# The state update's matmuls directly behind the turn in every unit of the Mamba-2 stage

## The chip, the cores and the metric

One Trainium2 chip, one of its cores. TensorE multiplies, VectorE, ScalarE and GpSimd do the elementwise work, SyncE issues most transfers. The metric is the time of the whole program on the device in microseconds (us), as the median of several executions; lower is better.

## The reference

Three blocks, each a residual layer over 1024 tokens of width 1024, run one behind the other. The change lies in the third block's Mamba-2 (SSD) mixer, and in the stage that computes it. Cut to that, the reference is:

```
h = rms_norm(x, norm_g);  proj = h @ w_in
xbc = silu(causal_depthwise_conv(xbc_raw, conv_w, conv_b))        # 4 taps
xs, bm, cm = split(xbc);  dt = softplus(dt_raw + dt_bias)
x_dt = xs * dt;  a_cs = cumsum(dt * a_head) within each chunk of 128 tokens
y_diag = sum over s <= l in the chunk of (C_l . B_s) exp(a_cs[l] - a_cs[s]) x_dt[s]
states[c] = sum over l in chunk c of B_l exp(a_cs[last] - a_cs[l]) x_dt[l]
state entering chunk c+1 = exp(a_cs[last of c]) * state entering c + states[c]
y_off = C_l . (state entering the chunk) * exp(a_cs[l])
y = (y_diag + y_off + xs * d_skip) * silu(z)
merged = g_sb * (y_sb @ w_out_sb) + g_ssd * (rms_norm(y) @ w_out_ssd) + g_rw * (y_rw @ w_out_rw)
x = x + merged @ w_o
```

There are 16 heads of 64 columns, two groups of 8 heads that share B and C (64 states each), and 8 chunks of 128 tokens. The gated output projections of the two other branches (`y_rw @ w_out_rw`, `y_sb @ w_out_sb`) need nothing of the Mamba-2 branch.

## The kernel before

Features lie on the 128 partitions and the 1024 tokens along them (`T` = 1024, `P` = `C` = 128, `NCH` = 8 chunks). Each stage is a set of per-engine programs written out by hand, in which each engine runs its own list in order, and waits on semaphores where it needs another engine's result. Nothing plans the order: it is the order of the calls.

The stage is `ssd_branch`. It runs 8 units `u`, each one pair of heads (128 feature rows). PSUM is held as four areas of 128 x 1024: `A` for the output, `F` for the projection that is computed alongside, `X` for the transposed input and `U` for the state sums. TensorE's list of a unit has five parts:

- `turn(u)` (L2814): 8 transposes that bring `xs` of the unit, once ScalarE has put the silu on it, into `X`.
- `fill(u, begin, end)` (L595, in `multiply_two`): matmuls `begin` to `end - 1` of the 48 that project one weight tile of the other two branches. Each is 128x128 by 512 tokens, and there are three for each product, because float32 is split in a high and a low part (`y_hi`, `y_lo`, and the stream's `w_hi`, `w_lo`). They fall in four sums of 12: part 0 first half of tokens, part 0 second half, part 1 first half, part 1 second half. `F` has room for two of them, so the third sum (from matmul 24) waits until ScalarE has copied the first out (`keep(u, 0)`), and the fourth (from matmul 36) until `keep(u, 1)` has copied the second. This is the wait on the semaphore `kept`.
- `update(u)` (L2826): 14 matmul instructions in the trace (7 chunks), the sums over each chunk of B times the decayed input, into `U`. It first waits for `x_ready(u)`, which VectorE gives at the end of `take_x(u)`.
- `products(u)` (L2838, L2840): the rest of the unit, 60 matmul instructions that need the state, the masked attention and a free `A`.
- `turn(u + 1)` ends the unit.

The order in the unit is written in the loop at L2843:

```
turn(0)
for u in range(units):
    first = 0 if u == 0 else 16
    fill(u, 0, first)
    update(u)
    fill(u, first, 48)
    products(u)
    if u + 1 < units:
        turn(u + 1)
```

So unit 0 has the update directly behind the turn already, and units 1 to 7 have 16 of the 48 projection matmuls between them.

VectorE's list of a unit: wait for the products of the unit before; `take_x` (L2939 scales the turned input by dt into `xdt`, L2942 by the decay into `xend`, two instructions each, then `x_ready`); `take_out` of the unit before (L2947); `advance_state` (L2953, L2955, L2958, which ends in `state_ready`); `gate(u, 0)` and `gate(u, 1)` (L2970, which multiply what `keep` copied by a gate); `finish` (L2975); `convolve(u + 1)` (L2920, L2922); `gate(u, 2)` and `gate(u, 3)`; `mask(u + 1)` (L2931). Behind `mask(4)` comes `cut_last(1)` (L2979), the last of four splits of the second branch's input into high and low part.

ScalarE's list of a unit: `clamp(u + 1, 0)` (L2866, 8 instructions); `keep(u, 0)` (L2885); `clamp(u + 1, 1)`, `decays(u + 1)` (L2874: a table load and two exponentials of 128x1024); `keep(u, 1)`; a table load and the silu of z (L2903); `keep(u, 2)`; `keep(u, 3)`; `round_y(1)` in unit 3 only (L2879); `silu(u + 1)` (L2858). Unit 7 has no clamp and no decays.

GpSimd splits the streamed weight tiles (`cut_tile`, L546 and L548), and in units 0 and 4 three of the four input rows (L2805). At unit 4 TensorE's first projection matmul also waits for that split (`y_cut`, in `fill`, wherever it is called with `begin` 0 and `end` above 0). SyncE's queue loads convolution inputs, z, decay rows, gates and one weight tile a unit, and stores the gated projections.

Of the kernel before, what the change touches and what calls it, by code (L numbers as in the profile page):

```python
# [2693 lines left out]
def ssd_branch(core, stream, base, xz_park, rows_dram, cols, ct, btok, cb, y, y_park, gate_park, out_park):  # L2694
# [4 lines left out]
    with Stage(core.nc, "ssd") as st:  # L2699
# [21 lines left out]
        def g_rows(u):  # L2721
            g = u // 4
            return slice(g * 64, g * 64 + 64)
# [84 lines left out]
        @block.tensor  # L2808
        def _(pe):
            def turn(u):  # L2810
                pe.wait_ge(activated, u + 1)
                for c in range(NCH):
                    s = slice(c * C, c * C + C)
                    ins = pe.transpose(X[:, s], xs[:, u % 2, s], core.ident[:, :])  # L2814
                ins.then_inc(x_turned, 1)

            def fill(u, begin, end):
                if u % 4 == 0 and begin == 0 and end:
                    pe.wait_ge(y_cut, u + 4)
                stream.multiply_two(pe, F, base + u, 0, 0, begin, end, (y_hi, y_lo), (kept, 4 * u + 1))  # L2820

            def update(u):
                pe.wait_ge(x_ready, u + 1)
                g = u // 4
                for c in range(NCH - 1):
                    ins = pe.matmul(U[g_rows(u), c * P:c * P + P], btok[:, c, g * 64:g * 64 + 64], xend[:, c, :],  # L2826
                                    start=True, stop=True)
                ins.then_inc(update_done, 1)

            def products(u):  # L2830
                r = g_rows(u)
                pe.wait_ge(state_ready, u + 1)
                pe.wait_ge(att_ready, u * 2 + 2)
                pe.wait_ge(out_free, u + 1)
                for sub, h in enumerate(heads):
                    for c in range(NCH):
                        s = slice(c * C, c * C + C)
                        ins = pe.matmul(A[h, s], xdt[:, c, h], att[:, u % 2, sub, s], start=True, stop=(c == 0))  # L2838
                        if c:
                            ins = pe.matmul(A[h, s], state[r, c, h], cdec[r, sub, s], start=False, stop=True)  # L2840
                ins.then_inc(out_done, 1)

            turn(0)  # L2843
            for u in range(units):
                first = 0 if u == 0 else 16
                fill(u, 0, first)
                update(u)
                fill(u, first, 48)
# [3 lines that stand above are left out]
# [755 lines left out]
```

## Time and profile before

| what | value |
|---|---|
| median of 3 executions | 5557.34 us (5556.14 to 5558.18) |
| the profiled execution, its own time | 5560.0 us |
| its span, first to last instruction | 5558.2 us |
| mean granted TensorE clock | 0.909 of full |
| TensorE matmul busy | 4837.1 us, 87% of the span |
| VectorE busy | 2445.5 us, 44% |
| ScalarE busy | 1167.5 us, 21% |
| GpSimd busy | 1266.0 us, 23% |

A busy share is over the whole program, which has some twenty stages with different limits; the change touches one of them, from about 5048 us (the first turn) to 5273 us (the last product), and there the timelines of single engines have to be read. A timeline row gives the start and the length of an instruction, or of a run of equal ones (x8), its line, what it writes and reads, and in brackets how long the engine sat idle before it and whose result ended the wait. Matmuls are pipelined: the time that one costs its engine is the distance between two starts, not its length. The granted clock is 1.00 at 2.4 GHz and 0.50 at 1.2 GHz; the third last column of a row by stretch is its mean.

### The profile page before, as it was taken

What the parts mean: (1) busy time and instruction counts of PE and PEld (TensorE: products, weight loads), DVE (VectorE), ACT (ScalarE), POOL (GpSimd) and SP (SyncE); (2) the same over time, 40 slices, a digit from 0 to 9 for tenths busy, and PEclk for the clock granted to TensorE, in tenths of its full rate; (3) what the DMA queues carried; (4) which work ended last, traced back from release to release, by engine and by line L of the source; (5) the groups of instructions that cost most, each with busy time, mean ns of one, the idle gap of its engine ahead of it and who ended that gap; (6) DMA issues with size and microseconds to landing.
All of it is one profiled execution on the core that took longest, in us unless ns stands there. A gap on an engine that the chain in (4) does not pass through costs nothing. (4 is left out here: it accounts for less than half of the span.)

```text
span 5558.2 us, 57845 instructions
## 1 busy us (share of the span) xinstructions
PE 4837.1 (87%) x22844; PEld 3780.5 (68%) x22844; DVE 2445.5 (44%) x2430; ACT 1167.5 (21%) x1396; POOL 1266.0 (23%) x616
## 2 busy tenths in 40 slices
PE   6999888859999998875886899989999899997977
PEld 4888776748777786764665686767768566665656
DVE  6544554341212213997443522324142244446853
ACT  3332331021111111110211211112121122224420
POOL 1222112212212121534121221213122111112221
PEclk8999997879999999987998988889898999997988
DMA  2111213011111111102231101101010111115541
GB/s 99 57 54 50 79 72 114 27 68 42 62 46 59 56 46 63 40 19 87 91 110 59 58 17 37 37 28 48 16 57 16 67 55 60 60 44 194 170 158 47
DMA packets 110978, 356.59 MB, mean 64 GB/s; under 512 B 12405, under 2 KB 13957, under 8 KB 110665
## 3 DMA queue, kind: packets, MB, share of 16 engines
q1 hardware_dynamic: 81952, 292.95, 15.2%
q10 hardware_dynamic: 28840, 60.91, 2.8%
q8 instruction: 148, 2.42, 0.2%
q14 instruction: 38, 0.30, 0.0%
HBM read 263.43 MB, written 90.39 MB: 64 GB/s over the span
## 5 line engine op out<-in xcount | busy, mean ns | idle before, releaser
L546 POOL CAST b_w_hi<-b_w 128x1024 fp32r<-128x1024 f32 x157 | 181.2, 1154 | 2451.3 <-PE ps L610 1914.2
L610 PE MATMUL ps<-h_hT_hi,b_w_hi 128*128 128x512 f32 x1216 | 528.4, 435 | 50.7 <-PEq L95 24.4
L610 PE MATMUL ps<-h_hT_lo,b_w_hi 128*128 128x512 f32 x1216 | 497.6, 409 | 0.0
L610 PE MATMUL ps<-h_hT_hi,b_w_lo 128*128 128x512 f32 x1216 | 496.4, 408 | 0.0
L548 POOL TENSOR_TENSOR b_w_lo<-b_w,b_w_hi 128x1024 fp32r<-128x1024 f32 x157 | 414.2, 2638 | 12.6
L610 PE MATMUL ps<-b_hT_hi,b_w_hi 128*128 128x512 f32 x848 | 357.2, 421 | 55.7 <-PEq L95 19.9
L478 PE MATMUL ps<-b_hi,ret_w_hi 128*128 128x512 f32 x768 | 303.7, 395 | 57.5 <-DVE ret_w_lo L445 29.5
L610 PEld LDWEIGHTS ps<-h_hT_hi,b_w_hi 128*128 128x128 f32 x1216 | 239.9, 197 | 154.1 <-issue 97.8
L610 PE MATMUL ps<-b_hT_lo,b_w_hi 128*128 128x512 f32 x848 | 342.1, 403 | 0.0
L610 PE MATMUL ps<-b_hT_hi,b_w_lo 128*128 128x512 f32 x848 | 341.5, 403 | 0.0
L478 PE MATMUL ps<-b_lo,ret_w_hi 128*128 128x512 f32 x768 | 300.9, 392 | 0.0
L610 PEld LDWEIGHTS ps<-h_hT_hi,b_w_lo 128*128 128x128 f32 x1216 | 238.9, 196 | 59.0
L610 PEld LDWEIGHTS ps<-h_hT_lo,b_w_hi 128*128 128x128 f32 x1216 | 240.6, 198 | 52.0 <-issue 4.3
L428 POOL CAST ret_w_hi<-ret_w 128x1024 fp32r<-128x1024 f32 x63 | 66.5, 1055 | 802.1 <-PE ps L478 392.8
L478 PE MATMUL ps<-b_hi,ret_w_lo 128*128 128x512 f32 x768 | 238.2, 392 | 0.0
L610 PEld LDWEIGHTS ps<-b_hT_hi,b_w_hi 128*128 128x128 f32 x848 | 167.1, 197 | 101.8 <-issue 32.2
L2098 DVE SCALAR_TENSOR_TENSOR xT<-b_pads,cols_sb,xT 128x1024 f32 (+1 forms) x134 | 209.0, 1575 | 0.0
L478 PEld LDWEIGHTS ps<-b_hi,ret_w_hi 128*128 128x128 f32 x768 | 145.8, 190 | 90.3 <-DVE ret_w_lo L445 31.0
L478 PE MATMUL ps<-b_hi,conv_w_hi 128*128 128x512 f32 x384 | 154.0, 401 | 57.8 <-ACT conv_sg L2145 38.2
L610 PEld LDWEIGHTS ps<-b_hT_hi,b_w_lo 128*128 128x128 f32 x848 | 166.2, 196 | 37.2
L610 PEld LDWEIGHTS ps<-b_hT_lo,b_w_hi 128*128 128x128 f32 x848 | 167.1, 197 | 34.4 <-issue 2.2
L478 PEld LDWEIGHTS ps<-b_lo,ret_w_hi 128*128 128x128 f32 x768 | 145.9, 190 | 29.7
(649 smaller groups left out, 10111.5 us busy)
## 6 DMA issues: line engine op xcount, KB each, us to landing
b_w<-in_w SPq DMA_DIRECT2D x157, 512.0 KB, 3.4
ret_w<-in_w SPq DMA_DIRECT2D x64, 512.0 KB, 3.3
scratch_x_park<-xT SPq DMA_DIRECT2D x24, 512.0 KB, 7.4
conv_w<-in_w SPq DMA_DIRECT2D x24, 512.0 KB, 3.3
xT<-scratch_x_park SPq DMA_DIRECT2D x16, 512.0 KB, 6.5
scratch_gate_park<-ret_gates_out ACTq DMA_DIRECT2D x16, 512.0 KB, 2.6
scratch_o_park<-ret_o ACTq DMA_DIRECT2D x16, 512.0 KB, 3.9
scratch_gate_park<-rw_fill_out ACTq DMA_DIRECT2D x32, 256.0 KB, 2.0
```

Source lines behind the costliest of these rows:

```text
L428: pool.tensor_copy(hi, w).then_inc(self.w_rounded, 1)
L478: ins = pe.matmul(out[:, t], w, y, start=start, stop=stop)
L546: pool.tensor_copy(hi, w).then_inc(self.rounded, 1)
L548: pool.tensor_tensor(lo, w, hi, ALU.subtract).then_inc(self.cut, 1)
L610: ins = pe.matmul(out[:, t], w, y, start=start, stop=stop)
L2098: ins = dve.scalar_tensor_tensor(a, x, wj, a, ALU.mult, ALU.add)
```

## The change

In TensorE's list of `ssd_branch` the number of projection matmuls ahead of the update becomes 0 in every unit, as it was in unit 0 alone. `fill(u, 0, 0)` issues nothing and waits for nothing; all 48 projection matmuls follow in `fill(u, 0, 48)`. No instruction is added or taken away, and no other engine's list changes.

```
             turn(0)
             for u in range(units):
-                first = 0 if u == 0 else 16
+                first = 0
                 fill(u, 0, first)
                 update(u)
                 fill(u, first, 48)
```

## Rows read from the trace of the kernel before

**Rows 1.** Busy time by stretch: us, the engines, TensorE clock, DMA share, GB/s.
```profile
5093.20:5142.40 49.20, 49.20 (x262) 33.76 (x261) 44.14 (x62) 27.40 (x53) 9.45 (x4) 1.00 0.72 237
...
5199.00:5273.30 74.30, 74.17 (x392) 50.83 (x392) 58.23 (x88) 30.79 (x57) 10.55 (x4) 1.00 0.49 162
```

**Rows 2.** TensorE's timeline, unit 1: start, us, instruction, idle before it.
```profile
5092.40 1.09 PE L2814 MATMUL ps<-c_ident_sb,ssd_xs 128*128 128x128 f32 x8
5093.24 0.48 PE L595 MATMUL ps<-ssd_o_hi,b_w_hi 128*128 128x512 f32 x1
...
5096.83 0.40 PE L595 MATMUL ps<-ssd_o_hi,b_w_hi 128*128 128x512 f32 x1
5097.15 1.74 PE L2826 MATMUL ps<-ssd_xend,ssds_btok 128*64 128x128 f32 x14
5098.83 0.51 PE L595 MATMUL ps<-ssd_o_lo,b_w_hi 128*128 128x512 f32 x1
...
5106.49 0.65 PE L2838 MATMUL ps<-ssd_att,ssd_xdt 128*64 128x128 f32 x4
...
5117.03 1.09 PE L2814 MATMUL ps<-c_ident_sb,ssd_xs 128*128 128x128 f32 x8
```

**Rows 3.** VectorE's timeline, unit 1.
```profile
5093.59 1.29 DVE L2939 TENSOR_TENSOR ssd_xdt<-ps,ssds_cols 128x512 f32<-128x512 f32 x2 [3.15 <-PE ps L2814]
5094.92 1.29 DVE L2942 TENSOR_TENSOR ssd_xend<-ssd_xdt,ssds_cols 128x512 f32<-128x512 f32 x2
...
5099.90 2.96 DVE L2958 SCALAR_TENSOR_TENSOR ssd_state<-ssd_state,ssd_erep,ps 64x64 f32<-64x64 f32 x12
```

**Rows 4.** VectorE's timeline, unit 7.
```profile
5249.70 1.29 DVE L2939 TENSOR_TENSOR ssd_xdt<-ps,ssds_cols 128x512 f32<-128x512 f32 x2 [1.57 <-PE ps L2814]
```

**Rows 5.** ScalarE's timeline, unit 1.
```profile
5096.38 0.60 ACT L2885 ACTIVATE ssd_ev<-ps 128x512 f32<-128x512 f32 x1 [1.37 <-PE ps L595]
5096.88 2.44 ACT L2866 ACTIVATE ssd_att<-ssd_crep,ssds_cols 128x128 f32<-128x128 f32 x8
...
5100.63 2.01 ACT L2874 ACTIVATE ssd_att<-ssd_att 128x1024 f32<-128x1024 f32 x2
5102.54 0.58 ACT L2885 ACTIVATE ssd_ev<-ps 128x512 f32<-128x512 f32 x1
```

**Rows 6.** TensorE's timeline, unit 0.
```profile
5077.42 0.39 PE L595 MATMUL ps<-ssd_o_hi,b_w_lo 128*128 128x512 f32 x1
5078.86 0.51 PE L595 MATMUL ps<-ssd_o_hi,b_w_hi 128*128 128x512 f32 x1 [1.05 <-ACT ssd_ev L2885]
```

**Rows 7.** VectorE's timeline, unit 4.
```profile
5171.97 1.21 DVE L2979 TENSOR_TENSOR ssd_o_lo<-ssd_y_sb,ssd_o_hi 128x1024 fp32r<-128x1024 f32 x1
...
5174.42 1.29 DVE L2942 TENSOR_TENSOR ssd_xend<-ssd_xdt,ssds_cols 128x512 f32<-128x512 f32 x2
```

**Rows 8.** TensorE's timeline, unit 4.
```profile
5173.24 0.79 PE L595 MATMUL ps<-ssd_o_hi,b_w_hi 128*128 128x512 f32 x1 [5.85 <-DVE ssd_o_lo L2979]
```

**Rows 9.** Busy time by stretch, unit 4.
```profile
5173.20:5178.20 5.00, 4.96 (x12) 3.90 (x13) 4.93 (x7) 0.00 (x0) 0.00 (x0) 0.50 0.00 0
```

**Rows 10.** TensorE's timeline, first block: four waits and what follows two.
```profile
186.40 1.09 PE L994 MATMUL ps<-c_ident_sb,hg_k 128*128 128x128 f32 x8 [3.17 <-DVE hg_k L1123]
...
190.76 1.50 PE L1000 MATMUL ps<-hg_v,hg_qs 128*128 128x128 f32 x12
...
300.29 1.75 PE L994 MATMUL ps<-c_ident_sb,hg_k 128*128 128x128 f32 x8 [3.15 <-DVE hg_k L1123]
...
415.85 1.28 PE L994 MATMUL ps<-c_ident_sb,hg_k 128*128 128x128 f32 x8 [3.16 <-DVE hg_k L1123]
...
421.83 0.38 PE L1000 MATMUL ps<-hg_v,hg_qs 128*128 128x128 f32 x2
...
531.37 1.09 PE L994 MATMUL ps<-c_ident_sb,hg_k 128*128 128x128 f32 x8 [3.16 <-DVE hg_k L1123]
```

**Rows 11.** Busy time by stretch, behind the second wait.
```profile
300.30:304.30 4.00, 4.00 (x15) 3.48 (x16) 0.00 (x0) 1.02 (x1) 0.00 (x0) 0.57 0.17 66
```

More of the change, by code:

```diff
@@ L2844, in _ @@
             for u in range(units):
-                first = 0 if u == 0 else 16
+                first = 0
                 fill(u, 0, first)
```

## The prediction

> **What bounds the kernel now.** I read the busy time by stretch first, then the timelines of single engines, and last the idle time behind waits like the one that the change makes. Between 5093.20 and 5142.40 (units 1 and 2) TensorE is busy 49.20 of 49.20 us, between 5199.00 and 5273.30 (units 5 to 7) 74.17 of 74.30, at a granted clock of 1.00, the 2.4 GHz level; VectorE is busy 44.14 of the 49.20 [rows 1]. So in seven of eight units TensorE has no hole: whatever holds it up adds to the end one for one. A unit takes 24.63 us from turn to turn, 5092.40 to 5117.03 [rows 2].
>
> The two other engines are ahead of it by margins that the reader should note. VectorE sat idle 3.15 us before take_x of unit 1 and 1.57 us before that of unit 7 [rows 3, 4]. The state is finished at 5099.90 + 2.96 = 5102.86, and the products that need it start at 5106.49, without an idle time of their own [rows 2, 3]: 3.6 us of margin.
>
> What now stands between turn and update? The 16 projection matmuls from 5093.24 to 5097.15, 3.91 us [rows 2]. In their shadow VectorE does take_x: it starts at 5093.59 and has xend at 5094.92 + 1.29 = 5096.21 [rows 3]. The update never waits, because it comes 0.94 us later. The 16 matmuls are the cover.
>
> **The change part by part.** *The update's wait.* It now stands alone behind the turn. A wakened TensorE starts 0.06 us behind VectorE's end (split done at 5171.97 + 1.21 = 5173.18, matmul at 5173.24) [rows 7, 8], so the update starts at 5096.27, where the projection started at 5093.24: 3.03 us without work. Behind it the work is the same: update 1.68 us (5097.15 to 5098.83), then 48 matmuls. The last 32 of them took 7.66 us up to the products (5098.83 to 5106.49); the first 16 take 15 steps in 3.59, of which 0.08 is start-up (the first is 0.48 long, the later ones 0.40), so a step is 0.234 and 16 more cost 3.74. From the old start of the projection to the products: before 13.25 us (5093.24 to 5106.49), after 3.03 + 1.68 + 7.66 + 3.74 = 16.11. That is 2.86 us a unit; one seam between two kinds of matmul goes, which is why it is less than 3.03. Bounds: 2.0 if take_x ran into the turn, 3.1 without the seam's gain.
>
> *A second wait, which the cover also hid.* ScalarE does keep(u, 0) at 5096.38, 3.14 us behind the start of the projection; behind that in its list stand the clamps (2.44), a table load and the exponentials (2.01), and only then keep(u, 1), from 5102.54 to 5103.12 [rows 5], 9.88 us behind the projection's start. The fourth sum (from matmul 36) needs it. Today the update's 1.68 us lies between matmuls 16 and 17, and matmul 36 gets there about when the copy is done. With the 48 in one piece it is due 0.08 + 36 x 0.234 = 8.50 us after the start, and can run at 9.88 + 0.05 = 9.93: 1.43 us of stall. Unit 0, whose order is already the new one, shows it: 1.05 us idle until ScalarE's ev [rows 6], where the step would have been 0.23 and was 1.44, so 1.21 lost. I take 1.43 for warm units, with 0 (the copy is no longer late) and 1.6 as ends. Unit 7 has no clamps and no decays, so none there.
>
> *Units 1, 2, 3, 5, 6:* 2.86 + 1.43 = 4.29, times 5 = 21.5 us. *Unit 7:* 2.86.
>
> *Unit 4* now starts its projection at 5173.24, after 5.85 us idle for the split of the second branch [rows 8]. VectorE makes that split before take_x, so xend comes at 5174.42 + 1.29 = 5175.71 [rows 7] and the update could start at 5175.77, 2.53 us later. Less the seam's 0.17, plus 1.43: 3.8 us. TensorE ran at 0.50 for the 5 us behind that wait [rows 9]; it would again, and I take the same price for it; if the low level also covers the update and more of the projection, up to 3 us come on top.
>
> *The clock.* The idle time of 3 us comes six times in warm stretches. The first block has four waits of this kind, of 3.15 to 3.17 us, each between full stretches. After the first the clock stayed up: transposes and 15 matmuls took from 186.40 to 190.76, 4.36 us. After the third the same work took 415.85 to 421.83, 5.98 us, and after the second the stretch shows a mean granted clock of 0.57, a fall to the 1.2 GHz level for most of it [rows 10, 11]; the fourth, the last row of rows 10, I count with these. So three falls in four, each 5.98 - 4.36 = 1.62 us. Here the idle time, counted as the profile does from the last transpose's end (5092.40 + 1.09), is 2.78 us, somewhat shorter. I take 4 falls in 6, 6.5 us, with 0 and 6 (9.7 us) as ends.
>
> By the Trainium skill (TensorE: Matmul & The Clock Gate, section on HAM oscillation) waits between bursts of matmuls bring the array back to half clock and the price is paid each time, but it puts the harm at idle gaps longer than these; read strictly, there would be no fall and the sum would be 6.5 us smaller. The first block's rows speak for falls behind waits this short, so they decide; the strict reading is the second rival.
>
> *What moves with it.* VectorE's gate(u, 1) waits for keep(u, 1), and finish, convolve and mask stand behind it. The copy now ends at 5103.12 [rows 5]; it would end at 5096.27 + 1.68 + 9.88 = 5107.83, at most 4.7 us later. The unit grows by 4.3 or more, so VectorE's idle time before the next take_x, 1.57 us or more [rows 3, 4], shrinks by 0.4 at worst and still hides the delay. SyncE's loads of gates, decay rows and z wait for these steps and have a longer unit to land in. GpSimd's split of the next weight tile starts at the end of the projection, as now.
>
> **Sum.** 21.5 + 2.86 + 3.8 + 6.5 = 34.6 us. Against the profiled execution's own 5560.0 us (span 5558.2, 1.8 outside it) this gives 5594.6. That execution lies 2.7 us above the median of 5557.34, so on the median it is 5592.
>
> **The rivals.** *The clock holds* in all or nearly all six waits (0 or 1 falls): 28.1 to 29.8, 5586. For it: the first of the four waits left no mark, and these are 0.4 us shorter. Against: three of four did.
>
> *The second wait is not there*, because the copies get ahead or a low clock behind the first wait delays matmul 36 by as much: 34.6 - 6 x 1.43 = 26, 5583. Against it stands unit 0 [rows 6].
>
> *The other side: the state decides.* If in truth the products wait for the state, the update 0.88 us earlier (5096.27 for 5097.15) hands it over sooner in seven units: up to 6.2 us faster, 5551. It decides from the point where the state is finished later than the projection. The rows say 5102.86 against 5106.49, so it would take 3.6 us of error.
>
> *Nothing happens:* TensorE finds xend ready, as if take_x were done within the turn, or the order in the list has no effect. 5557. Against it: VectorE starts 1.19 us after the turn does and needs 2.62 [rows 2, 3].
>
> *VectorE becomes the bound,* if the late gate pushes convolve and mask beyond the next turn by more than the 1.6 us: 1 us more a unit, 5600 or more. Against: the unit grows as fast as the delay.
>
> **How the numbers follow.** Forecast (2 to 6 falls, both waits) 0.62; clock holds 0.20; no second wait 0.10; VectorE bound 0.04; nothing happens 0.02; state decides 0.02. Predicted 5592. The forecast's own range is 5557.3 + 28.1 + 3.2 = 5588.6 to 5557.3 + 28.1 + 9.7 = 5595.1, and the longer low clock in unit 4 adds up to 3. The range takes in the two next rivals and that: 5579 to 5600. A change under 0.2%, 11 us, can hardly be told from none here; slower by more 0.96, within it 0.02, faster 0.02.
>
> **What would show it.** In the profile of the changed kernel the update should be behind about 2.8 us of idle time that ends on VectorE's xend, in each of units 1 to 3 and 5 to 7; the projection matmul 36 behind about 1.2 us that ends on ScalarE's ev, in units 1 to 6; the unit should take 28.9 us with the clock up, 30.5 with a fall. TensorE's busy share of the stretch falls from 1.00 to about 0.86. Rows of 0.63 us per matmul behind the update would show the falls. It is wrong if the update shows no wait, if matmul 36 has none, if the clock stays at 1.00 throughout, or if VectorE's idle time before take_x is gone.

## The result and the profile after

| | before | after |
|---|---|---|
| median of 4 executions each, us | 5556.74 (5554.88 to 5558.18) | 5596.03 (5588.67 to 5603.17) |
| ratio, 95% interval | | 1.0071 (1.0053 to 1.0088) |
| second comparison, us | 5559.06 (19 executions) | 5595.12 (5 executions) |
| ratio, 95% interval | | 1.0061 (1.0047 to 1.0075) |
| profiled execution's own time, span | 5560.0, 5558.2 | 5603.17, 5601.4 |

Slower, by 36 to 39 us or 0.6 to 0.7%; the forecast was 34.6 us more, 5592.

Busy time by stretch of the changed kernel, units 1 to 3 and then units 5 to 7 (the columns are those of [rows 1]):

```profile
5097.70:5189.70 92.00, 79.81 (x392) 55.21 (x391) 67.59 (x91) 44.95 (x82) 18.45 (x8) 0.94 0.57 189
5226.60:5314.00 87.40, 76.48 (x376) 53.02 (x376) 58.47 (x87) 30.80 (x57) 9.64 (x4) 0.94 0.40 138
```

TensorE was busy 49.20 of 49.20 us in [rows 1]; it is now busy 79.81 of 92.00, and its granted clock is 0.94 where it was 1.00. VectorE is busy for 58.47 us in units 5 to 7, where it was 58.23: the same work, spread over more time. So TensorE has got holes, and part of the lost time is a slower clock.

TensorE's timeline, unit 1, answers to [rows 2]:

```profile
5097.73 1.09 PE L2814 MATMUL ps<-c_ident_sb,ssd_xs 128*128 128x128 f32 x8
5101.60 3.25 PE L2826 MATMUL ps<-ssd_xend,ssds_btok 128*64 128x128 f32 x14 [2.78 <-DVE ssd_xend L2942]
5104.78 0.60 PE L595 MATMUL ps<-ssd_o_hi,b_w_hi 128*128 128x512 f32 x1
...
5114.83 0.50 PE L595 MATMUL ps<-ssd_o_hi,b_w_hi 128*128 128x512 f32 x1 [1.29 <-ACT ssd_ev L2885]
...
5128.37 1.09 PE L2814 MATMUL ps<-c_ident_sb,ssd_xs 128*128 128x128 f32 x8
```

The unit goes from 5097.73 to 5128.37, 30.64 us for 24.63. Two waits are new: 2.78 us for VectorE's xend in front of the update, 1.29 us for ScalarE's ev in front of matmul 36. The third change is in the lengths: from update to projection 5101.60 to 5104.78, 3.18 us for 1.68. Over these 3.2 us the mean granted clock is 0.50: TensorE ran at the 1.2 GHz level behind the idle time.

VectorE's and ScalarE's timelines of the same unit answer to [rows 3] and [rows 5]:

```profile
5098.93 1.29 DVE L2939 TENSOR_TENSOR ssd_xdt<-ps,ssds_cols 128x512 f32<-128x512 f32 x2 [3.15 <-PE ps L2814]
5100.25 1.29 DVE L2942 TENSOR_TENSOR ssd_xend<-ssd_xdt,ssds_cols 128x512 f32<-128x512 f32 x2
```

```profile
5108.05 0.60 ACT L2885 ACTIVATE ssd_ev<-ps 128x512 f32<-128x512 f32 x1 [7.71 <-PE ps L595]
5108.54 2.44 ACT L2866 ACTIVATE ssd_att<-ssd_crep,ssds_cols 128x128 f32<-128x128 f32 x8
...
5114.20 0.58 ACT L2885 ACTIVATE ssd_ev<-ps 128x512 f32<-128x512 f32 x1
```

VectorE does take_x at the same distance from the turn (1.20 us for 1.19), xend ends at 5101.54 and the update starts 0.06 later. ScalarE's two copies start 6.15 us apart (6.16 in [rows 5]), and TensorE goes on 0.05 us behind the second.

Unit 4, TensorE and VectorE, answers to [rows 7, 8]:

```profile
5199.20 3.25 PE L2826 MATMUL ps<-ssd_xend,ssds_btok 128*64 128x128 f32 x14 [8.46 <-DVE ssd_xend L2942]
```

```profile
5195.41 1.21 DVE L2979 TENSOR_TENSOR ssd_o_lo<-ssd_y_sb,ssd_o_hi 128x1024 fp32r<-128x1024 f32 x1
...
5197.85 1.29 DVE L2942 TENSOR_TENSOR ssd_xend<-ssd_xdt,ssds_cols 128x512 f32<-128x512 f32 x2
```

The wait is 8.46 us for xend, where it was 5.85 for the split. Unit 4 lasts 36.95 us (turn to turn, 5189.65 to 5226.60), where it lasted 32.96 (5166.30 to 5199.26).

The length of the whole stage can be compared between kernels without what the rest of the program does. It is taken from the first turn on TensorE to the last take_out on VectorE, which starts when the last product is done. In the changed kernel:

```profile
5053.25 1.97 PE L2814 MATMUL ps<-c_ident_sb,ssd_xs 128*128 128x128 f32 x8 [19.53 <-ACT ssd_xs L2858]
```

```profile
5316.91 1.28 DVE L2947 SCALAR_TENSOR_TENSOR ssd_xs<-ssd_xs,cols_sb,ps 128x1024 f32<-128x1024 f32 x1 [9.16 <-PE ps L2840]
```

That is 263.66 us. In the kernel before these rows start at 5047.91 and 5273.21, 225.30 us apart. The stage grew by 38.4 us. The first turn comes 5.3 us later than in the kernel before, with the same code ahead of it, so these 5.3 us are not the change's.

### The profile page after: what moved, and what is told of

Its sections match the earlier page's. It is cut to its first block and busy times, and to the rows that moved or that the text cites. A ratio compares the mean times of both kernels' runs of the same rounds, so it can differ in the third digit from the quotient of the medians.

```text
span 5601.4 us, 57845 instructions
## 1 busy us (share of the span) xinstructions
PE 4852.8 (87%) x22844; PEld 3794.7 (68%) x22844; DVE 2450.6 (44%) x2430; ACT 1167.5 (21%) x1396; POOL 1267.1 (23%) x616
## 5 line engine op out<-in xcount | busy, mean ns | idle before, releaser
L610 PEld LDWEIGHTS ps<-b_hT_lo,b_w_hi 128*128 128x128 f32 x848 | 168.0, 198 | 34.6 <-issue 2.2
```

What stands on the lines that cost most here:

```text
L610: ins = pe.matmul(out[:, t], w, y, start=start, stop=stop)
```

## The experiments

The table has the stage length of each kernel's profiled execution, its difference to 225.30, and the timed comparison with the kernel before. The times that were expected are worked out from about 5557 us for the kernel before; it ran at 5559.06 and 5560.50 beside these kernels, so the differences are what to compare.

| kernel | stage us | difference | median us | before, us | ratio, 95% interval |
|---|---|---|---|---|---|
| changed kernel | 263.66 | +38.4 | 5596.03 | 5556.74 | 1.0071 (1.0053 to 1.0088) |
| again | 262.70 | +37.4 | 5595.12 | 5559.06 | 1.0061 (1.0047 to 1.0075) |
| busy_wait | 253.26 | +28.0 | 5586.20 | 5559.06 | 1.0044 (1.0031 to 1.0058) |
| copy_first | 246.41 | +21.1 | 5578.93 | 5559.06 | 1.0033 (1.0023 to 1.0043) |
| busy_wait_copy_first | 240.71 | +15.4 | 5574.24 | 5559.06 | 1.0026 (1.0017 to 1.0036) |
| cover8 | 240.53 | +15.2 | 5572.94 | 5560.50 | 1.0022 (1.0013 to 1.0031) |
| cover12 | 225.56 | +0.3 | 5556.88 | 5560.50 | 0.9996 (0.9987 to 1.0005) |
| split_early | 218.94 | -6.4 | 5553.58 | 5560.50 | 0.9987 (0.9978 to 0.9996) |
| split_early_copy_first | 218.42 | -6.9 | 5553.11 | 5560.50 | 0.9986 (0.9977 to 0.9995) |

A stage length is one execution's. Unit 0, where no edit but the one to ScalarE's copy changes the order, took 44.5 us in five profiles and 43.8 in two (the changed kernel again, and cover8), so differences under 1 us are not read from the stage alone.

My theory was three terms: the update's wait, the wait for the second copy, and clock falls behind the first. The rivals were that one of them does not exist, or that they hide each other.

### The changed kernel again

No edit.

> The changed kernel once more, unchanged. Theory (three terms: the update's wait 2.9 us a unit, the wait for the second copy 1.4 us in six units, and clock falls of up to 1.6 us behind each of six waits, which differ from execution to execution): between 5585 (no fall) and 5595 (six falls) plus or minus what the rest of the program varies by (3 us), so the executions spread over 10 us or more where those of the kernel before spread over 3. Rival (the clock adds the same amount each time): the spread is as small as before's.

Measured: 5595.12 us (5592.94 to 5597.99), and the kernel before beside it 5550.35 to 5565.92. The part on the spread was wrong: it was 5 us for the changed kernel and 16 for the kernel before, and 14.5 and 3.3 in the first comparison, so a spread of whole executions says nothing on this stage. The profile by unit does. Units 1, 2 and 5, busy time by stretch:

```profile
5093.50:5125.00 31.50, 27.44 (x132) 19.08 (x130) 22.25 (x31) 13.73 (x26) 4.82 (x2) 0.89 0.58 184
5125.00:5155.60 30.60, 26.53 (x132) 18.10 (x130) 22.24 (x31) 13.73 (x26) 4.83 (x2) 0.94 0.58 189
5223.70:5252.70 29.00, 24.94 (x131) 16.95 (x130) 22.60 (x31) 13.72 (x26) 4.82 (x2) 1.00 0.62 198
```

The same instructions take 31.5, 30.6 and 29.0 us, at a mean granted clock of 0.89, 0.94 and 1.00. With the clock up the unit is 29.0 us; a fall adds 1.5 to 2.5 us. In this execution five of six waits of 2.78 us had a fall behind them. In the first profile it was all six, and units 1, 2, 3, 5 and 6 took 30.6 us each.

### Matmuls of no use in the wait

```
                 fill(u, 0, first)
+                if u % 4:
+                    pe.wait_ge(stream.cut, base + u + 1)
+                    for n in range(11):
+                        pe.matmul(U[:, 0:512], stream.w_hi[:, (base + u) % stream.RING, 0:P],
+                                  y_hi[:, 0, 0:512], start=True, stop=True)
                 update(u)
```

> The changed kernel with 11 matmuls of no use (128x128 by 512, into the update's own area of PSUM, overwritten by it) between turn and update in units 1, 2, 3, 5, 6 and 7. They last 11 x 0.234 = 2.6 us of the 3.03 us that TensorE waits. Theory (clock falls behind idle time): the update starts no later, the granted clock stays 1.00 in these units, and the time is 5556.7 + 28.1 = 5585 with a spread of about 3 us. Rival 1 (the clock adds nothing, the whole loss is waits): same time and spread as the changed kernel, 5596. Rival 2 (useless matmuls delay the update): each unit 0.3 us or more longer than the wait, 5587 or above.

Measured: 5586.20 us, 1.0044, so 27.1 us over the kernel before for 28.1 expected. `u % 4` leaves units 0 and 4 as they are. TensorE's timeline of unit 1 and the stretch of units 1 to 3:

```profile
5095.06 1.09 PE L2814 MATMUL ps<-c_ident_sb,ssd_xs 128*128 128x128 f32 x8
...
5098.93 1.74 PE L2826 MATMUL ps<-ssd_xend,ssds_btok 128*64 128x128 f32 x14 [0.22 <-DVE ssd_xend L2947]
...
5110.55 0.50 PE L595 MATMUL ps<-ssd_o_hi,b_w_hi 128*128 128x512 f32 x1 [1.30 <-ACT ssd_ev L2890]
...
5124.08 1.09 PE L2814 MATMUL ps<-c_ident_sb,ssd_xs 128*128 128x128 f32 x8
```

```profile
5095.06:5182.10 87.04, 82.52 (x424) 56.69 (x423) 67.23 (x91) 44.98 (x82) 18.36 (x7) 1.00 0.60 200
```

The update still starts 3.87 us behind the turn, as in the changed kernel, so nothing was saved in waiting. But 0.22 us of idle time is left of 2.78, the clock stays at 1.00 (in units 5 to 7 too), the update takes its old 1.74 us, and the unit is 29.02 us. The stage is 28.0 us longer than before; the two waits alone were worked out as 28.1. It lacks 10.4 and 9.4 us against the changed kernel's two profiles. Unit by unit, 9.5 and 8.7 of these lie in the six units with the useless matmuls, and are the price of six and five falls. The rest lies in units 0 and 4, whose code is the same: in unit 4 the mean clock over the first 5 us of the update and what follows was 0.52 and 0.50 in the changed kernel and 0.72 here, and the unit took 36.95, 37.51 and 36.06 us. The other rival, useless work that delays the update, did not show.

### The second copy ahead of the exponentials

```
                 if u + 1 < units:
                     clamp(u + 1, 1)
-                    decays(u + 1)
                 keep(u, 1)
+                if u + 1 < units:
+                    decays(u + 1)
```

> The changed kernel with ScalarE's second copy, keep(u, 1), ahead of decays(u + 1) in its list. Theory: matmul 36 no longer waits (idle 1.29 us gone in units 1 to 6), 6 x 1.43 = 8.6 us less than the changed kernel, so about 5587; the update's wait of 2.78 us stays in the profile. Rival (VectorE's chain or the mask decides as soon as the copy doesn't): idle time of the same size appears in front of the products or the turn and the time stays at 5596.

Measured: 5578.93 us, 1.0033, which is 16.2 us under the changed kernel by the medians; the stage is 17.2 us shorter than in its first profile. That is twice the 8.6 expected. The update of unit 4, then unit 6:

```profile
5187.73 3.25 PE L2826 MATMUL ps<-ssd_xend,ssds_btok 128*64 128x128 f32 x14 [5.82 <-DVE ssd_xend L2943]
...
5240.45 1.09 PE L2814 MATMUL ps<-c_ident_sb,ssd_xs 128*128 128x128 f32 x8
...
5244.32 1.74 PE L2826 MATMUL ps<-ssd_xend,ssds_btok 128*64 128x128 f32 x14 [2.78 <-DVE ssd_xend L2943]
...
5267.93 1.09 PE L2814 MATMUL ps<-c_ident_sb,ssd_xs 128*128 128x128 f32 x8
```

The update's 2.78 us stay, no row at matmul 36 has an idle time, and the unit is 27.48 us: 29.03 less 1.55. In five units that is 7.8. Three things come on top. Unit 0, which the edit helps as well, is 1.3 us shorter. Unit 4 takes 32.16 us (5180.81 to 5212.97) for 36.95, of which 1.55 are the second copy and 2.6 the wait in front of the update, 5.82 us for 8.46. In unit 3 VectorE begins the gate that waits for the second copy 15.3 us ahead of unit 4's turn, and not 13.6. Its row in this kernel, and in the changed kernel:

```profile
5165.48 0.69 DVE L2971 TENSOR_TENSOR ssd_sg<-ssd_sg,ssd_ev 128x512 f32<-128x512 f32 x1 [2.12 <-ACT ssd_ev L2885]
```

```profile
5176.09 0.69 DVE L2970 TENSOR_TENSOR ssd_sg<-ssd_sg,ssd_ev 128x512 f32<-128x512 f32 x1 [5.45 <-ACT ssd_ev L2885]
```

From there to the end of xend its list takes 22.2 us for 23.1. The third thing is that four of six waits had a clock fall behind them, two fewer. The next kernel takes the clock out.

### Both

> Both: the 11 useless matmuls in the wait, and keep(u, 1) ahead of decays(u + 1). Theory: only the update's wait is left, 6 x 2.86 + 2.4 in unit 4 = 19.5 us over the kernel before, so 5576. Rival (terms overlap, a clock fall hides the second wait or the other way round): the two gains do not add, 5580 or above.

The edits are the two above. Measured: 5574.24 us, 1.0026, so 15.2 us over the kernel before for 19.5 expected. Unit 1:

```profile
5091.08 1.09 PE L2814 MATMUL ps<-c_ident_sb,ssd_xs 128*128 128x128 f32 x8
...
5094.95 1.74 PE L2826 MATMUL ps<-ssd_xend,ssds_btok 128*64 128x128 f32 x14 [0.22 <-DVE ssd_xend L2948]
...
5118.55 1.09 PE L2814 MATMUL ps<-c_ident_sb,ssd_xs 128*128 128x128 f32 x8
```

27.47 us a unit with the clock up. The stage is 12.55 us shorter than with the useless matmuls alone: 7.8 in units 1, 2, 3, 5 and 6, 1.4 in unit 0, 3.4 in unit 4 (32.65 for 36.06). Against the kernel before a unit has 27.48 - 24.63 = 2.85 us more, for 2.86 forecast; six of them less the 1.4 of unit 0 and 0.3 in unit 4 are the 15.4 of the stage. So the terms add, and what is left is the update's wait alone. The 19.5 expected left out what units 0 and 4 gain.

### The cover made shorter

```
-                first = 0 if u == 0 else 16
+                first = 0 if u == 0 else 12
```

> The kernel before with 12 instead of 16 projection matmuls ahead of the update in units 1 to 7. Theory (the cover has to last 3.03 us): 0.08 + 12 x 0.234 = 2.9 us and a seam cover it, the update waits 0.1 us or not at all, keep(u, 0) and keep(u, 1) come at the same time as with 16, the second wait stays away and the time is that of the kernel before within 2 us. Rival (any update ahead of matmul 16 brings the second wait, since less work lies between copy and matmul 36): 1.2 us idle at matmul 36 in six units, 7 us more.

and the same with 8:

> The same with 8 matmuls ahead of the update. Theory: they cover 0.08 + 8 x 0.234 = 1.95 of 3.03 us, so the update waits some 0.8 us by the profile (1.0 us of time) in units 1 to 3 and 5 to 7, and not in unit 4; the update now stands ahead of matmul 12, so keep(u, 0) comes late and matmul 36 waits the full 1.3 us in units 1 to 6. No clock falls behind waits this short. Sum 6 x 1.0 + 6 x 1.43 = 14.6 us over the kernel before. Rival (second wait only with no cover at all): 6 us over. Rival (the clock falls here too): 20 us or more over, with a granted clock under 1.00 in units 1 to 3.

Measured: with 12, 0.9996 (0.9987 to 1.0005), no change. With 8, 1.0022, 12.4 us over the kernel before by the medians and 15.2 by the stage; 14.6 were expected. TensorE's timeline of unit 1, with 12 and with 8:

```profile
5091.50 1.10 PE L2814 MATMUL ps<-c_ident_sb,ssd_xs 128*128 128x128 f32 x8
...
5095.38 1.74 PE L2826 MATMUL ps<-ssd_xend,ssds_btok 128*64 128x128 f32 x14
...
5116.19 1.09 PE L2814 MATMUL ps<-c_ident_sb,ssd_xs 128*128 128x128 f32 x8
```

```profile
5094.12 1.09 PE L2814 MATMUL ps<-c_ident_sb,ssd_xs 128*128 128x128 f32 x8
...
5097.99 1.74 PE L2826 MATMUL ps<-ssd_xend,ssds_btok 128*64 128x128 f32 x14 [0.93 <-DVE ssd_xend L2942]
...
5107.75 0.50 PE L595 MATMUL ps<-ssd_o_hi,b_w_hi 128*128 128x512 f32 x1 [1.29 <-ACT ssd_ev L2885]
...
5121.29 1.09 PE L2814 MATMUL ps<-c_ident_sb,ssd_xs 128*128 128x128 f32 x8
```

With 12 the update starts 3.88 us behind the turn and never waits; the unit takes 24.69 us, 0.06 more than with 16. With 8 it starts 3.87 behind the turn too, but with 0.93 us of idle time, and matmul 36 waits 1.29. The unit, 27.17 us, holds both, 2.5 us more than with 16 for 2.4 expected, and no clock fall: the update still takes 1.74, and the mean granted clock of units 1 to 3 is 1.00. Unit 4 is 2.2 us longer, unit 7 1.0. So the update cannot start earlier than 3.87 us behind the turn whatever stands in between; the first wait is absent with 12 matmuls and there with 8, and the second is absent with 12 and there in full with 8. That the second needs no empty cover decides against its rival.

### Towards a faster kernel: the split of unit 4

```
                 gate(u, 3)
-                if u + 1 < units:
-                    mask(u + 1)
                 if u == 3:
                     cut_last(1)
+                elif u + 1 < units:
+                    mask(u + 1)
```

and `if u == 4: mask(u)` behind `advance_state(u)`, in the kernel before with its 16 matmuls.

> The kernel before (16 matmuls ahead of the update) with VectorE's cut_last(1) right behind gate(3, 3) and mask(4) moved from there to behind advance_state(4). TensorE's 5.85 us wait in unit 4 was for cut_last, which stood behind 5.33 us of mask. Theory: the wait shrinks to about 1 us (GpSimd's part of the split ends at 5166.2, cut_last 1.2 us behind the gates), and the clock does not fall there, 5 + 2 = 7 us less than the kernel before. Rival (VectorE and GpSimd slow each other, so cut_last takes as long as the mask did): 2 us less or nothing. Rival (the mask is now late for the products of unit 4): idle time in front of them of the size of what was won.

Measured: 5553.58 us against 5560.50, 0.9987 (0.9978 to 0.9996); the stage 6.4 us shorter. TensorE and VectorE at unit 4, and the stretch from its turn on:

```profile
5162.04 0.50 PE L595 MATMUL ps<-ssd_o_hi,b_w_hi 128*128 128x512 f32 x1 [1.44 <-DVE ssd_o_lo L2979]
```

```profile
5159.93 2.05 DVE L2979 TENSOR_TENSOR ssd_o_lo<-ssd_y_sb,ssd_o_hi 128x1024 fp32r<-128x1024 f32 x1
...
5172.47 2.36 DVE L2931 TENSOR_TENSOR ssd_att<-ssd_att,ssds_cb 128x1024 f32<-128x1024 f32 x2
```

```profile
5159.50:5186.00 26.50, 25.01 (x132) 17.00 (x131) 25.96 (x34) 13.83 (x26) 9.22 (x4) 1.00 0.65 220
```

The wait is 1.44 us where it was 5.85 [rows 8], the granted clock is 1.00 where it was 0.50 behind it [rows 9], and no idle time stands in front of the products. The mask, now at 5172.47, takes 2.36 us. In the kernel before it took 5.33, in a stretch in which GpSimd was splitting a weight tile:

```profile
5166.72 5.33 DVE L2931 TENSOR_TENSOR ssd_att<-ssd_att,ssds_cb 128x1024 f32<-128x1024 f32 x2
```

```profile
5167.77 3.20 POOL L548 TENSOR_TENSOR b_w_lo<-b_w,b_w_hi 128x1024 fp32r<-128x1024 f32 x1
```

The rival was right in part: VectorE's split, which now stands beside that work of GpSimd, takes 2.05 us where it took 1.21 [rows 7], and the wait is 1.44 us for the 1 us expected.

With ScalarE's copy ahead as well:

> The same with keep(u, 1) ahead of decays(u + 1) on ScalarE. Theory: unit 0's wait at matmul 36, 1.2 us, goes as well, so 8 us less than the kernel before; the other units had no wait there with 16 matmuls ahead of the update and gain nothing. Rival: decays 0.6 us later delay the mask and eat the 1.2 us.

Measured: 0.9986 (0.9977 to 0.9995), which the timing cannot tell from the last. The stage is 0.5 us shorter, not 1.2: unit 0 is 1.3 us shorter, unit 4 0.7 longer. Unit 4:

```profile
5165.03 0.50 PE L595 MATMUL ps<-ssd_o_hi,b_w_hi 128*128 128x512 f32 x1 [0.77 <-DVE ssd_o_lo L2980]
...
5169.56 1.74 PE L2826 MATMUL ps<-ssd_xend,ssds_btok 128*64 128x128 f32 x14 [0.54 <-DVE ssd_xend L2943]
...
5190.34 1.09 PE L2814 MATMUL ps<-c_ident_sb,ssd_xs 128*128 128x128 f32 x8 [0.70 <-ACT ssd_xs L2858]
```

Unit 0's wait is gone, the wait for the split is down to 0.77, but 0.54 us at the update and 0.70 us in front of the next turn (for ScalarE's silu) have come in. Either version is faster than both kernels of this case. Against the kernel before it is 0.13 to 0.14%, and the interval lies below 1 by little.

## Why the prediction was right

**The update's wait.** 2.78 us idle in each of units 1 to 3 and 5 to 7, the update 3.87 us behind the turn, as worked out (5096.27 less 5092.40). Alone, in the kernel with both edits, it costs 2.85 us a unit for a forecast of 2.86.

**The second wait.** Forecast 1.43 us of time, seen as 1.29 idle in units 1 to 6; taking the copy forward removed 1.55 us from the unit.

**Unit 4.** 36.95 and 37.51 us in the changed kernel's two profiles for 32.96 in the kernel before, 4.0 and 4.6 more; forecast 3.8. With the same code in this unit it was 3.1 more in busy_wait, where the low clock ended sooner.

**The two waits together.** Forecast 28.1, and 28.0 measured where the clock was held up. That the two agree to 0.1 us is in part luck: units 1, 2, 3, 5 and 6 took 22.0 us more for 21.5, and unit 4 took 3.1 for 3.8.

**The clock.** Here the term was too small. I took four falls in six and 1.62 us each, 6.5 us; the two profiles show six and five, and 9.5 and 8.7 us. The mechanism and, but for one fall of 2.5 us, the price are those forecast; the count was low. The fourth wait of [rows 10], which I counted as a fall, was one: the transposes and 15 matmuls behind it took 5.96 us (531.37 to 537.33). That the idle time is 0.4 us shorter than in [rows 10] did not spare it. The strict reading of the Trainium skill (TensorE: Matmul & The Clock Gate, section on HAM oscillation), that gaps this short do no harm, is contradicted, if a gap is the idle time of the profile, by falls behind 15 of 18 waits of 2.78 us in three profiles (the changed kernel's two, and copy_first); that the price is paid at every return, as it says, agrees. Behind waits of 0.93 us (with 8 matmuls) there was none in six. Eight transposes stand beside every one of the long waits, ahead of it here and behind it in [rows 10]; no run takes them apart from the wait.

**The rivals.** The clock did not hold. The second wait exists. The state did not decide: the update 0.9 us earlier gave nothing back. VectorE did not become the bound: its idle time before take_x is 3.15 us in unit 1, as before, and 2.0 in units 2, 3 and 5 to 7. I had let it shrink by up to 0.4 us; in unit 7, where it was shortest, it grew from 1.57 to 2.02.

**The sum.** The stage grew by 38.4 and 37.4 for a forecast of 34.6. The difference of the medians was 39.3 in one comparison and 36.1 in the other. A unit took 29.0 us with the clock up and 30.6 with a fall, for 28.9 and 30.5 forecast, and TensorE's busy share was 79.81 / 92.00 = 0.87 for 0.86. The 38.4 are the 28.0 of the two waits, 9.5 for six falls and 0.9 for the longer low clock of unit 4, so what the sum owed to the clock, it underrated by 3 to 4 us.

## What to carry to other kernels

Before a dependent step is moved directly behind the one that feeds it, measure how long the hand-over through the other engine takes (here 3.0 us) and how much independent work must stay in between (12 matmuls of 0.234 us; 8 were too few, 16 no better). The same filler can hide a second thing, here a copy that stood behind 5.7 us of other work in ScalarE's list, and a wait that costs 2.85 us cost about 1.6 us more through the clock wherever the clock fell. When a wait cannot be filled, look at what stands ahead of its releaser in that engine's list: moving one split ahead of a mask brought 6.4 us.

## What was not expected of the hardware

The spread of whole executions is larger than three or four of them show: the kernel before lay between 5554.88 and 5558.18 in 4 executions, and between 5550.35 and 5565.92 in 19. In the profiled ones the first turn of this stage, with the same program ahead of it, came at 5041.17, 5047.91 and 5053.25 us. Where these 12 us arise was not looked into; the comparison of stage lengths is free of it. VectorE's two mask operations of 128x1024 took 5.33 us in the kernel before, beside GpSimd's split of a weight tile, and 2.36 in split_early, with no GpSimd work beside them.
